# Turning and splitting keys and queries once, in the input stage, two heads per transpose, instead of per head in prompt attention

## What is computed

```python
h = rmsnorm(x, norm_g)
proj = h @ w_in                      # pool, q, k, v, gates, forget logits, conv
q = rmsnorm(q.reshape(B, T, 8, 64), q_norm_g)
k = rmsnorm(k.reshape(B, T, 8, 64), k_norm_g)
s = einsum('bqhd,bkhd->bhqk', q, K) * 64 ** -0.5
s = s + Fq[..., None] - Fk           # cumulative log forget gates
p = softmax(where(k_pos <= q_pos, s, -inf))
o = einsum('bhqk,bkhd->bqhd', p, V)  # then gates, pool and conv branches, x + mixed @ w_out
```

## Time and profile before

| | |
|---|---|
| median of 3 runs | 1553.63 us (1553.26 to 1553.94) |
| the profiled execution | 1556.87 us, its span 1555.1 us |
| mean granted TensorE clock | 0.994 |
| input stage, from the start to about | 721 us |
| prompt attention, about | 721 to 1197 us |

### The profile page before, as it was taken

How to read it: one execution, slowest core, us unless ns; L and a number is a source line. 1 busy time by engine, 2 the same in 40 slices (tenths; PEclk the granted TensorE clock), 3 DMA queues, 4 the chain that set the end, 5 groups by cost and what they waited for, 6 DMA issues and landing times.

```text
span 1555.1 us, 24722 instructions
## 1 busy us (share of the span) xinstructions
PE 1511.0 (97%) x9212; PEld 1338.6 (86%) x9212; DVE 894.9 (58%) x2139; ACT 652.2 (42%) x1371; POOL 462.4 (30%) x742
## 2 busy tenths in 40 slices
PE   8999999999999999998999999999998899989998
PEld 8997888878799999998988888888887788878887
DVE  3333112242453613224988988988987778798663
ACT  5443021121211101014877877877876444433220
POOL 2110005555510100213344444444432445303221
PEclk9999999999999999999999999999999999999999
DMA  4533123122110201502233233233324566634442
GB/s 160 157 109 97 43 85 104 48 75 75 42 55 21 72 20 38 81 25 51 50 68 62 52 75 64 50 79 64 50 59 149 179 223 225 221 137 149 163 156 89
DMA packets 177160, 144.65 MB, mean 93 GB/s; under 512 B 103759, under 2 KB 136432, under 8 KB 177040
## 3 DMA queue, kind: packets, MB, share of 16 engines
q1 hardware_dynamic: 174528, 134.08, 29.3%
q10 hardware_dynamic: 2448, 8.91, 1.4%
q0 software_dynamic: 64, 0.07, 0.1%
HBM read 106.50 MB, written 36.53 MB: 92 GB/s over the span
## 4 chain that ended last, share of the span: by engine, by line
PE 72%; DVE 8%; POOL 8%; issue 5%; ACT 4%; DMA 2%; SPq 0%; POOLq 0%; DVEq 0%; ACTq 0%
PE banks L1002 18%; PE banks L996 13%; PE banks L2662 9%; PE banks L1634 6%; PE banks L1625 4%; PE banks L1620 4%; PE banks L1650 4%; PE banks L1651 3%; POOL in_h_rstd L549 3%; POOL in_out L554 3%; DVE sa_v_lo L2008 2%; PE banks L2635 2%; PE banks L1603 2%; PE banks L2111 2%; PE banks L2092 2%
## 5 line engine op out<-in xcount | busy, mean ns | idle before, releaser
L996 PE MATMUL banks<-in_w_hi,in_xt_hi 128*128 128x512 f32 (+1 forms) x680 | 240.6, 354 | 3.7 <-DVE in_w_lo L717 2.0
L996 PE MATMUL banks<-in_w_hi,in_xt_lo 128*128 128x512 f32 (+1 forms) x680 | 238.1, 350 | 0.0
L996 PE MATMUL banks<-in_w_lo,in_xt_hi 128*128 128x512 f32 (+1 forms) x680 | 237.3, 349 | 0.0
L1524 DVE CUSTOM_DVE_ANT_0 pa_s_ring<-banks,pa_f_b 128x512 f32<-128x512 f32 (+2 forms) x320 | 193.2, 604 | 36.9 <-PE banks L1625 34.1
L1572 DVE TENSOR_TENSOR pa_pt_lo<-banks,pa_pt_hi 128x512 fp32r<-128x512 f32 (+2 forms) x320 | 193.0, 606 | 21.1 <-ACT pa_pt_hi L1503 18.5
L1002 PE MATMUL banks<-in_xt_hi,in_w_hi 128*128 128x384 f32 (+1 forms) x576 | 192.8, 335 | 1.1 <-DVE in_w_lo L723 0.7
L1002 PE MATMUL banks<-in_xt_hi,in_w_lo 128*128 128x384 f32 (+1 forms) x576 | 189.3, 329 | 0.0
L1503 ACT ACTIVATE pa_pt_hi<-banks 128x512 fp32r<-128x512 f32 (+2 forms) x320 | 166.6, 534 | 53.6 <-PE banks L1634 52.7
L1002 PE MATMUL banks<-in_xt_lo,in_w_hi 128*128 128x384 f32 (+1 forms) x576 | 189.0, 328 | 0.0
L1634 PE MATMUL banks<-ident,pa_s_ring 128*128 128x128 f32 x1088 | 174.3, 275 | 9.7 <-DVE pa_pt_lo L1572 4.4
L1650 PE MATMUL banks<-pa_pt_hi,pa_vs 128*128 128x256 f32 x576 | 164.0, 301 | 0.4 <-DVE pa_parts L1552 0.3
(11 more groups left out here) (301 smaller groups left out, 2922.4 us busy)
## 6 DMA issues: line engine op xcount, KB each, us to landing
sa_k_c<-in_cache_k_dram SPq DMA_DIRECT2D x8, 2048.0 KB, 9.0
sa_v_c<-in_cache_v_dram SPq DMA_DIRECT2D x8, 2048.0 KB, 8.2
out_dram<-in_out SPq DMA_DIRECT2D x34, 256.0 KB, 2.0
out_dram<-op_x ACTq DMA_DIRECT2D x17, 512.0 KB, 3.3
op_x<-in_x_prompt_dram SPq DMA_DIRECT2D x16, 512.0 KB, 4.0
in_x<-in_x_prompt_dram SPq DMA_DIRECT2D x14, 512.0 KB, 3.6
pa_f_b<-scratch_f SPq DMA_DIRECT2D x28, 256.0 KB, 5.0
in_w_raw<-in_w_in_dram SPq DMA_DIRECT2D x24, 256.0 KB, 3.7
```

The lines of the kernel that those rows point to most:

```text
L996: mm = pe.matmul(ps[:, u % NBANK, 0:n], tile_of(xa, t)[:, k, :], wa[:, k, c0:c0 + n], start=(k == 0 and q == 0), stop=(k == KT - 1 and q = ...
L1524: done = dve.tensor_tensor_reduce(scores_of(j)[:, b * P:(b + nb) * P], ps_s[:, (h * NQD + at) % 3, 0:nb * P], f_b[h % 2][:, b * P:(b + nb) ...
```

## The change

Every prompt tile of KEY and QRY, once POOL has multiplied the gain into its slot, is transposed by PE straight from `out` in four blocks of 128x128 (two heads in one) into the banks `ps_x`, in the middle of the unit two tiles later; ACT copies the high part, DVE makes the low part, and SP stores both to a scratch `qk_t_all` of 4 x 512 rows (key high, key low, query high, query low) and 2048 columns. The prompt tiles of q are not stored as rows any more. Prompt attention loads per head the halves of `ks`, `q_h`, `q_l` from that scratch, directly in their final form; `q_h` and `q_l` hold a whole head, twice. `k_raw`, `q_raw`, `split`, `ident_r` and the 96 steps are gone. Waits are added where the new buffers overlap others: ACT waits for all turned stores before the pool phase, DVE before it writes into the same bytes.

```diff
 def input_stage
-    past_u = m.at(R + 4384, "past_u", [NB * HIST, DP])
+    past_u = m.at(207936, "past_u", [NB * HIST, DP])
+    t_hi = [m.at(n, f"t_hi{n}", [P, DA], F32R) for n in (R, R + 4352)]
+    t_lo = [m.at(n, f"t_lo{n}", [P, DA], F32R) for n in (R + 2048, 205888)]
...
     def on_sp, store
                 if ph == QRY:
+                    if t < PT:
+                        return
                     rows = q_all[t * P:(t + 1) * P, :]
...
+        def store_turned(n):
+            sp.wait_ge(t_l, n + 1)
+            kind, t = divmod(n, PT)
+            for part, buf in enumerate((t_hi, t_lo)):
+                rows = qk_t_all[(2 * kind + part) * DA:(2 * kind + part + 1) * DA, t * P:(t + 1) * P]
+                sp.dma_start(rows.rearrange("(a p) r -> p a r", p=P),
+                             buf[n % 2][:, :].bitcast(F32).rearrange("p (a r) -> p a r", r=P)).then_inc(t_stored[n % 2], 16)
...
                 store_before(ph, t)
+                n = to_turn(NT * (ph - KEY) + t - 3)
+                if n is not None:
+                    store_turned(n)
             store(ph, LAST_T)
         load_slab(0)
         load_slab(1)
+        store_turned(N_TURNED - 2)
+        store_turned(N_TURNED - 1)
...
     def on_act
+        def high_turned(i):
+            n = to_turn(i)
+            if n is None:
+                return
+            act.wait_ge(t_ps, n + 1)
+            if n >= 2:
+                act.wait_ge(t_stored[n % 2], 32 * (n // 2))
+            act.activation(t_hi[n % 2][:, :], ps_x[:, n % 2, :], ACT.Copy).then_inc(t_h, 1)
         for ph in (KEY, QRY):
             for t in range(LAST_T):
                 square_qk(ph, t)
+                high_turned(NT * (ph - KEY) + t - 2)
             for k in range(KT):
                 split_w(KT * (ph + 1) + k)
             square_qk(ph, LAST_T)
+            high_turned(NT * (ph - KEY) + LAST_T - 2)
+        high_turned(2 * NT - 2)
+        for i in range(2):
+            act.wait_ge(t_stored[i], 16 * N_TURNED)
...
     def on_dve
+        def low_turned(i):
+            n = to_turn(i)
+            if n is None:
+                return
+            dve.wait_ge(t_h, n + 1)
+            if n == 1:
+                dve.wait_ge(f_stored, 64)
+            dve.tensor_tensor(t_lo[n % 2][:, :], ps_x[:, n % 2, :], t_hi[n % 2][:, :].bitcast(F32),
+                              ALU.subtract).then_inc(t_l, 1)
         for ph in (KEY, QRY):
             for t in range(LAST_T):
                 norm_qk(ph, t)
+                low_turned(NT * (ph - KEY) + t - 2)
             for k in range(KT):
                 split_w(KT * (ph + 1) + k)
             norm_qk(ph, LAST_T)
+            low_turned(NT * (ph - KEY) + LAST_T - 2)
+        low_turned(2 * NT - 2)
         link(dve.memset(u[:, :, 0:HIST], 0.0))
+        dve.wait_ge(t_stored[0], 16 * N_TURNED)
...
     def on_pe
+        def turn_out(i):
+            n = to_turn(i)
+            if n is None:
+                return
+            ph, t = (KEY, QRY)[i // NT], i % NT
+            pe.wait_ge(qk_out, i + 1)
+            if n < 2:
+                pe.wait_ge(f_copied, 1)
+                pe.wait_ge(t_copied, 3)
+            else:
+                pe.wait_ge(t_l, n - 1)
+            for a in range(DA // P):
+                mm = pe.transpose(ps_x[:, n % 2, a * P:(a + 1) * P], out[:, slot(ph, t)[0], a * P:(a + 1) * P],
+                                  ident[:, :])
+            mm.then_inc(t_ps, 1)
         for ph in (VAL, KEY, QRY):
             for t in range(NT):
                 for k in range(KT):
+                    if ph != VAL and k == KT // 2:
+                        turn_out(NT * (ph - KEY) + t - 2)
...
         for c in range(NCK + 1):
             channel_unit(POOL, c, 0, 0)
             if c == 0:
+                turn_out(2 * NT - 2)
                 pe.wait_ge(small_pc, 16 * (3 + CONV_W))
...
                 if j:
-                    if c == 0:
-                        pe.wait_ge(ends_c, 2)
-                        pe.wait_ge(mixed, 2 * (NCK + 1))
-                    after_chunk(c)
...
 def prompt_attention
-    k_raw = [m.at(n, f"k_raw{n}", [P, NJ, HD]) for n in (0, 81920)]
-    q_raw = [m.at(n, f"q_raw{n}", [P, NJ, HD]) for n in (4096, 86016)]
+    q_h = [m.at(n, f"q_h{n}", [P, SEQ], F32R) for n in (24576, 49152)]
+    q_l = [m.at(n, f"q_l{n}", [P, SEQ], F32R) for n in (0, 57344)]
...
+        def load_parts(h, dst, kind, parts):
+            for half, part in enumerate(parts):
+                at = (2 * kind + part) * DA + h * HD
+                sp.dma_start(dst[h % 2][half * HD:(half + 1) * HD, :].bitcast(F32),
+                             qk_t_all[at:at + HD, :]).then_inc(qk_in[h % 2], 16)
+        def load_keys_and_q_high(h):
+            load_parts(h, ks, 0, (0, 1))
+            load_parts(h, q_h, 1, (0, 0))
+        def load_q_low(h):
+            load_parts(h, q_l, 1, (1, 1))
...
                 if h + 2 < H and j == 14:
-                    load_qk(h + 2)
+                    sp.wait_ge(scored, (h + 1) * NQD)
+                    load_keys_and_q_high(h + 2)
+                    load_q_low(h + 2)
...
-        def split_step(h, s): ...
-        def prep_copy(h, s): ...
-        def prep(h, s): ...
...
         def score(h, j, n):
-            if n == 0 and j % 4 == 0:
-                pe.wait_ge(prep_done, h * NPREP + 3 * c + 3)
+            if n == 0 and j == 0:
+                pe.wait_ge(qk_in[h % 2], 96 * (h // 2 + 1))
-            pe.matmul(out, q_h[:, (4 * h + c) % NQC, j % 4, :], keys, start=True, stop=False)
+            pe.matmul(out, q_h[h % 2][:, j * P:(j + 1) * P], keys, start=True, stop=False)
...
+        pe.wait_ge(consts, 4)
+        source.banks_read(pe)
         for j in range(AHEAD):
             score(0, j, 0)
         for h in range(H):
             for j in range(NJ):
-                for step in prep_at(h, j):
-                    prep(*step)
```

More of the change, by code:

```diff
@@ L234, in input_stage @@
     qk_out = m.sem("qk_out_done")
+    t_ps = m.sem("qk_transposed")
+    t_h = m.sem("qk_transposed_hi_done")
+    t_l = m.sem("qk_transposed_lo_done")
+    t_stored = [m.sem(f"qk_transposed_stored{i}") for i in range(2)]
     stored = [m.sem(f"rows_stored{i}") for i in range(NOUT)]
@@ L328, in slot, with rows_stored, to_turn @@
         return n % NOUT, n // NOUT
+    def rows_stored(ph, t):
+        at, use = slot(ph, t)
+        return sum(n % NOUT == at for n in range(min(NT * ph + t, NT * QRY)))
+    def to_turn(i):
+        if i < 0 or i >= 2 * NT or i % NT == PT:
+            return None
+        return PT * (i // NT) + i % NT
+    N_TURNED = 2 * PT
+    N_STORED = [sum(n % NOUT == i for n in range(NT * QRY)) + (i == slot(QRY, LAST_T)[0]) for i in range(NOUT)]
     def columns(c):
@@ L1148, in mix_landed, with banks_read, prompt_attention @@
             eng.wait_ge(mix_stored[i], 16 * (N_MIX // 4))
+    def banks_read(eng):
+        for part in range(4):
+            wait_freed(eng, unit(CONV1, NCK, part))
+        eng.wait_ge(mixed, 2 * (NCK + 1))
     def states_landed(eng):
         eng.wait_ge(states_out, 64)
-    return Input(on_sp, on_pool, on_act, on_dve, on_pe, chunk_dead, mix_landed, states_landed)
-def prompt_attention(plan, source, ident, q_all, k_all, v_all, gate_all, f_all, att_all):
+    return Input(on_sp, on_pool, on_act, on_dve, on_pe, chunk_dead, banks_read, mix_landed, states_landed)
+def prompt_attention(plan, source, ident, qk_t_all, v_all, gate_all, f_all, att_all):
     NJ = PT
@@ L1316, in store @@
                          ob[:, n % NOB, :, :]).then_inc(stored[n % NOB], 16)
-        if first:
-            load_qk(0)
+        if first == 1:
             load_v(0)
+            load_q_low(0)
             load_f(0, 0, NJ)
@@ L1323, in on_sp @@
             return
-        load_qk(1)
+        if first == 2:
+            load_keys_and_q_high(0)
+            return
+        load_keys_and_q_high(1)
+        load_q_low(1)
         for h in range(H):
@@ L1369, in on_pool @@
                            base=0, pattern=[[-1, P]], channel_multiplier=1).then_inc(consts, 1)
-        def split_step(h, s):
-            c, kind = s // 3, s % 3
-            at = h * NPREP + s
-            tiles = slice(4 * c, 4 * c + 4)
-            slot = split[:, at % NSLOT, :, :, :]
-            if s == 0:
-                pool.wait_ge(qk_in[h % 2], 32 * (h // 2 + 1))
-            after(pool, prep_t, at + 1 - NSLOT)
-            if kind == KIND_K:
-                high(slot[:, :, 0, :], k_raw[h % 2][:, tiles, :]).then_inc(q_hi, 1)
-                pool.wait_ge(q_hi, h * 4 + c + 1)
-                pool.tensor_tensor(slot[:, :, 1, :], k_raw[h % 2][:, tiles, :], slot[:, :, 0, :].bitcast(F32),
-                                   ALU.subtract).then_inc(split_done, 1)
-            elif kind == KIND_QH:
-                high(slot[:, :, 0, :], q_raw[h % 2][:, tiles, :])
-                high(slot[:, :, 1, :], q_raw[h % 2][:, tiles, :]).then_inc(split_done, 1)
-            else:
```

(28 more changed lines are left out.)

129 lines of the change are left out of this document (34 added, 95 removed).

## The result

The changed kernel takes **1539.42 us** (median of 4 runs, 1538.24 to 1539.99); the kernel before took 1553.79 beside it (4 runs). The profiled execution took 1539.99 us, its span is 1538.3. Its span is 16.8 us shorter than that of before, 2.4 more than the medians say: the profiled execution of before lay 3.2 us above its median, the one of after 0.6.

A forecast was written before the change was run, and what follows sets the result against it. PE was taken as the bound, level with DVE mid-head in attention. Terms: -5.3 - 12.6 - 10.5 - 2.7 + 14.1 + 0.6 + 8.9 + 2.5 = -5.0 us, from 1553.63 to 1548.6; range 1542.0 to 1557.0.

The forecast's parts named there:

- Part 1: Last conv chunks: the deleted transposes were all on PE's path, -5.3 us; ACT's last gate costed at nothing.
- Part 2, middle: Attention, tiles 4 to 12 of heads 0 to 6: nine deleted transpose groups worth 1.8 us a head, -12.6.
- Part 2, ends: Attention, last three deleted groups of each of heads 0 to 6: 1.5 us a head, -10.5.
- Part 2, head 0: Attention, head 0: PE's 1.75 us wait for POOL's key split and about 1.0 of lost clock go, -2.7.
- Part 3: Key and query phases: 4 added transposes for each of 32 tiles, +14.1 us, and +0.6 at the phase ends.
- Part 4: Before the pool phase: PE waits +8.9 us through a new drain of turned stores, then loses +2.5 to lower clock.
- B: Rival on the drain before the pool phase: it hides, wait 1 or less, net -15.5 us, 1538; chance 0.12.
- D: Rival on the ends of heads: nothing won because ACT's exps set the pace, +5.5 us, 1559.1; chance 0.14.
- units at 6.02: Sign in the key and query phases: PE units 6.02 us apart for 5.58, with 4 transposes in their middle.
- a wait of 6 to 12 us ended by DVE: Sign before the pool phase: PE waits 6 to 12 us ahead of the first pooled product, ended by DVE.
- clock 0.50 behind it: Sign after PE's wait ahead of the first pooled product: the granted clock is at 0.50.
- heads 55.8 us apart: Sign in prompt attention: successive heads 55.8 us apart, for 59.1 before.

The follow-up runs named there:

- e12: The changed kernel with a bank of the ring passed over, without transpose or copy, at tiles 4 to 12 of heads 0 to 6: 1544.83 us.
- e3: The changed kernel with one extra ACT copy of 128x512, SBUF to SBUF, at tiles 13 to 15 of heads 0 to 6: 1543.74 us.
- e2: The changed kernel with 4 extra PE transposes, no bank more and no copy, at tiles 13 to 15 of heads 0 to 6: 1544.16 us.
- e5: The changed kernel with both 4 extra PE transposes and an ACT copy, but no extra bank, at tiles 13 to 15 of heads 0 to 6: 1546.73 us.
- e6: The changed kernel with a bank of the ring passed over, without transpose or copy, at tiles 13 to 15 of heads 0 to 6: 1555.52 us.
- e11: The changed kernel with each of the 32 groups of 4 float32 transposes in the key and query phases issued twice: 1553.17 us.
- e7: The changed kernel with the odd low-part buffer moved, no ACT wait for turned stores, and DVE's history copy one chunk later: 1529.59 us.
- e8: The changed kernel with the four stores of the last two turned tiles issued ahead of the first two weight slabs: 1538.21 us.

## Why the prediction was wrong, step by step

**Part 1** (-5.3): -4.8, right within 0.6. Behind it PE now waits 0.5 us for ACT's last gate, which had been costed at nothing.

**Part 2, middle** (-12.6): right. The intervals of all heads are those of the old head 7, as the earlier trace rows promised; e12 adds that a third of the price was the ring's.

**Part 2, ends** (-10.5): **this step failed**, by 7.0 of the 9.4 us between -5.0 and -14.4. "Bounds per head: nothing ... and 2.2 us (1.0 at this step, 0.6 each at the other two)", and of that 1.5 was taken, since "ACT alone gets rid of three copies of some 0.5 us". Measured is 2.5, above even the upper bound. The step from 2.2 down to 1.5 was the larger error: it priced the groups by the work that was deleted. Three such copies by themselves are worth 0.5 us (e3), PE's transposes 0.8 (e2), both together 1.1 (e5), and the position in the ring, with no work at all, the whole 2.5 (e6): once the bank is missing, the work adds nothing. The earlier trace rows had the cost in full view at one tile, and the forecast named the bank, but gave it no term of its own. The rows of tiles 13 and 15 of the same head, which stood beside it, were not used:

```profile
886.86 0.46 PE L1603 MATMUL banks<-pa_ident_r,pa_split 128*128 128x128 f32 x4
887.30 0.63 PE L1634 MATMUL banks<-ident,pa_s_ring 128*128 128x128 f32 x4
...
896.18 0.51 PE L1603 MATMUL banks<-pa_ident_r,pa_split 128*128 128x128 f32 x4 [0.23 <-DVE pa_pt_lo L1572]
896.78 0.63 PE L1634 MATMUL banks<-ident,pa_s_ring 128*128 128x128 f32 x4
```

That is 0.44 at tile 13 and 0.83 at tile 15 (wait and group), 2.3 in all with the 1.0 of tile 14: by these rows the term was -16. The bare waits of e6 are 0.86, 1.08 and 0.83, and of the last the changed kernel still has a part, at the same tile 15:

```profile
897.52 0.63 PE L1642 MATMUL banks<-ident,pa_s_ring 128*128 128x128 f32 x4 [0.32 <-DVE pa_pt_lo L1597]
```

So 2.45 of e6's 2.77 us are new, which is the 2.5 a head.

**Part 2, head 0** (-2.7): -3.5. The 1.75 us stall and the whole 1.7 us of clock together are 3.45, so it looks as if all of the clock was on the path and not 1.0 of it (not tried by itself). No wait for keys is left in attention, and no wait for the new loads, though `q_l` takes 13.2 us to land: the work of the head before covers them.

**Part 3** (+14.7): +13.4, the row's 0.42 for 0.44, and the boundaries cost nothing: PE idles 0.23 us ahead of the pool phase for 0.46 in the earlier trace rows, presumably because its own added transposes cover DVE's added low part. By the Trainium skill's 81 ns ("TensorE: Matmul & The Clock Gate", section "Back-to-back issue gap") the part would have been 10.4, as an estimate; this trace has 0.42 us for four, 105 ns each, and e11 118 ns for each further one.

**Part 4** (+8.9 and +2.5): the chain was right link by link, +7.35 and +2.6. The stores landed 9.6 us after SP came free for 10.2 forecast, and PE came for the product 0.46 later than thought. ACT and DVE needed 3.5, as the forecast's own 0.5 and 2.9 say; it added them wrongly: 439.1 + 0.5 + 2.9 is 442.5 and not 443, and PE's 433.13 + 0.88 + 0.3 is 434.3, so its own terms give a wait of 8.2 for the 8.9 written. The slip made the forecast 0.7 slower and moves it to -5.7 when put right; it is not what failed. e7 shows the two terms as a sum, 9.8.

**The rivals.** B (1538) came nearest in time and was wrong in its mechanism: the drain did not hide. D, nothing won at the ends of heads, erred in the same term and the same direction as the forecast, by 2.5 us a head for 1.0; ACT at 3.97 of 4 us was no evidence for it. The range was also said to hold most of D's side, but D starts at 1556.7 and the range ends at 1557.0. What was listed as a sign of the forecast (units at 6.02, a wait of 6 to 12 us ended by DVE, clock 0.50 behind it, no wait at tile 4 of head 0) all appeared, and of "heads 55.8 us apart" the profile showed 54.8: the one sign that bore on the failed term.

## What to carry to other kernels

Count buffers of a ring by uses, not by the work in them: here a use that did nothing at all cost as much as a full one, where it stood ahead of work that was then one buffer short, and 0.06 us or less at eight of the nine places in the middle of a head (e12). To price such a use before it is deleted, read the distance between the milestones of every place where it stands, not of one: in the kernel before only 0.49 and 0.23 us of the 2.5 stood as idle time of PE. That the cost follows the length of the chain behind the buffer (here an exponential, a copy and a subtraction) is argued from the timelines, not shown by a run that changes the chain. And a wait for a whole set of stores at a change of phase is worth one look at which bytes really overlap: here one buffer 4 KB further on and one copy later gave 9.8 us.

## What the runs showed of the hardware that was not expected

POOL shuts DVE out. A DVE operation on 64x16 elements, 0.17 us alone, lasted 1.78 beside POOL's multiplication of a slab, and one of 64x384 lasted 2.20 for 0.62 (e8): POOL's two multiplications take 3.98 us together, so, if they are equally long, they end near 449.92 and at 451.91, and the two DVE operations end 0.2 and 0.4 us behind them. The Trainium skill says in "SBUF — State Buffer", section "SBUF: two separate sides", that the pair of ports shared by the two engines is an exclusive lock held for a whole instruction and that the loser blocks fully, for a DVE operation with two inputs in SBUF beside a POOL operation that reads SBUF, as both are here; this trace agrees. It is how a landing 3.2 us earlier brought nothing.

Issuing a store is not of one price. SP takes 0.36 to 0.43 and 0.51 to 0.57 us for the two stores of nearly every turned tile in the key and query phases, and 0.82 to 1.31 for each of the last four, issued while 1 MB of slabs is on its way. Ahead of the slabs (e8) the same four take 0.43, 0.58, 0.56 and 0.87.

After a stall of 7.35 us PE's clock stayed at the lower level until about 458, 5 us after work had resumed; it cost 2.6 us. The same kernel without the stall shows clock 1.00 through the whole stretch.
